# Dense networks: two pairs of steps by seven block products, with weight sums on GpSimd

## Chip, cores and metric

The kernel runs on 1 core of one Trainium2 chip. The metric is device microseconds (us) of one execution; lower is better.

## What is computed

Two transformer blocks over 256 tokens of width 1024, in float32. The first has a state space mixer, attention and a mixture of 32 experts; the second has two layers, each a dense network, a mixer, and a second dense network, so there are four dense networks in all. The change lies in those four:

```
def swiglu(x, w_gate, w_up, w_down):
    return (jax.nn.silu(x @ w_gate) * (x @ w_up)) @ w_down
...
    h = h + 0.5 * swiglu(rms_norm_2(h, ffn_norm[layer, 0]), ffn_w_gate[layer, 0], ffn_w_up[layer, 0], ffn_w_down[layer, 0])
```

`x` has 256 rows of 1024; the weights are 1024 x 2816, 1024 x 2816 and 2816 x 1024.

## The kernel before

**Steps.** A dense network q (0 to 3) is cut into 11 steps m (`FFN_STEPS`) of 256 hidden columns. Step m has one item of the ring: 128 partitions x 6144 columns, 3 MB, in three pieces of 2048 columns. Piece 0 and piece 1 hold the gate and up weights of the first and the second half of the 1024 inputs (each four blocks of 512 columns, 256 gate and 256 up), piece 2 holds the down weights.

**Split products.** Every factor is split into a high part and a low part (type fp32r), and `split_product` (line 2272) issues three matmuls of 512 columns: high x high, high x low, low x high (lines 2274, 2276 and 2275 in the profile). ScalarE makes the high part of a weight piece by a copy (`ffn_weights_high`, line 2896, profile line 2906), and DVE the low part by a subtraction with both operands in SBUF (`ffn_weights_low`, line 2833, by `low_part`, profile line 2280). High and low parts lie in the rooms of `ffn_hi` and `ffn_lo`, four rooms of 2048 columns each. In the text a form is the high and low part of one weight block.

**PE's order** (`ffn_tensor`, line 2735). `gate_up(m, 0)`, `gate_up(m, 1)`: 24 matmuls each, 8 blocks of 128 inputs x 2 token tiles x 3. `turn(m)`: four transposes of the gated rows (profile line 2785). `down(m)`: 24 matmuls that add to four banks held through the network. The loop is

```
        if m < FFN_LAST:
            gate_up(m + 1, 0)
            turn(m)
            gate_up(m + 1, 1)
        down(m)
```

**DVE and ScalarE** run hand-written orders of their own (`ffn_vector`, line 2841, and `ffn_scalar`, line 2909): per step three conversions, the silu on ScalarE (line 2920), the product with the up half on DVE (line 2854), and the split of the transposed rows (`turned_high`, line 2927, `turned_low`). Each engine runs its list in order and waits on semaphores, which count ends of instructions.

**Loads.** SyncE issues the items in the order of `plan_ring` (line 197) into three slots, item by item in turn. An item's load waits until the low part of the down weights of the item before it in that slot is made (`ffn_down_lo`). Loads and items keep that order into the next stage: after the first network come the entry weights `hy0`, `hy1`, after the second network the third one's items follow at once, and ScalarE and DVE make the third network's first form inside the second's last step.

**GpSimd** has little to do: it turns query and key rows (`mla_rows`, `nsa_query_rows`, `nsa_key_rows`; lines 724 to 730) in the mixers, and nothing in the dense networks.

**Last.** The gain of the last norm is loaded into `final_row`, 1024 columns of the tile `work`, after `out_ready` 12.

Of the kernel before, what the change touches and what calls it, by code (L numbers as in the profile page):

```python
# [56 lines left out]
FFN_STEPS = DFF2 // STEP_COLS  # L57
ALPHA = 1.702
# [42 lines left out]
def offsets(table):  # L101
# [80 lines left out]
def plan_ring(sig):  # L182
# [2537 lines left out]
def ffn_room(m, piece):  # L2720

    return 3 if piece == 2 and m == FFN_LAST else piece


def ffn_acts(k, part, m):

    return k[part if m < FFN_LAST else part.replace("act", "last")][:, :, :]


def down_free(q, m):  # L2730

    return downs_at(q, 0 if m == FFN_LAST else m)


def ffn_tensor(k, pe, q, nxt=None):
    s = k["sig"]
    base = FFN_STEPS * q
    half_kt = KT // 2

    def first_half():  # L2740
# [5 lines left out]
        def term(h, w):  # L2746
            for kt in range(half_kt):
                for t in range(TT):
                    mm = pe.matmul(k["ps"][2 * (base % 2) + t][:, :], k[h][:, kt, t * P:(t + 1) * P], k[w][:, 0, kt * 512:(kt + 1) * 512], start=h == "hT_hi" and w == "ffn_hi" and kt == 0, stop=False)  # L2749
            return mm  # L2750
# [3 lines left out]
        pe.wait_ge(s["ffn_w_lo"], 2 * base + 1)  # L2754
# [4 lines left out]
    def gate_up(m, piece):  # L2759
        n = base + m  # L2760
        pe.wait_ge(s["ffn_w_hi"], 2 * n + piece + 1)
# [3 lines left out]
        pe.wait_ge(s["ffn_w_lo"], 2 * n + piece + 1)  # L2765
# [4 lines left out]
        if piece == 0 and n >= 1:  # L2770
            pe.wait_ge(s["act_ready"], n)
        for kk in range(half_kt):
            kt = piece * half_kt + kk
            w = [k[part][:, piece, kk * 512:(kk + 1) * 512] for part in ("ffn_hi", "ffn_lo")]
            for t in range(TT):
                h = [k[part][:, kt, t * P:(t + 1) * P] for part in ("hT_hi", "hT_lo")]
                mm = split_product(pe, k["ps"][2 * (n % 2) + t][:, :], h, w, kt == 0, kt == KT - 1)
        mm.then_inc(s["gu_ready"], 1)

    def turn(m):  # L2780
        n = base + m
        pe.wait_ge(s["gu_drained"], n + 3)
        for ff in range(STEP_TILES):
            for t in range(TT):
                mm = pe.transpose(k["ps"][2 * (n % 2)][:, (ff * TT + t) * P:(ff * TT + t + 1) * P], k["sg"][:, t * STEP_COLS + ff * P:t * STEP_COLS + (ff + 1) * P], con(k, "ident"))  # L2785
        mm.then_inc(s["actT_ready"], 1)

    def down(m):
        n = base + m
# [27 lines left out]

    gate_up(0, 0)
    gate_up(0, 1)
    for m in range(FFN_STEPS):  # L2820
        if m < FFN_LAST:
            gate_up(m + 1, 0)
            turn(m)
            gate_up(m + 1, 1)
        down(m)


def downs_at(q, m):
# [12 lines left out]
def ffn_vector(k, dve, q, gain):
# [3 lines left out]
    def weights_low(m, piece):  # L2845
        ffn_weights_low(k, dve, q, m, piece)

    def swiglu(m):
        n = base + m
        banks = [k["ps"][2 * (n % 2) + t] for t in range(TT)]  # L2850
        dve.wait_ge(s["sig_ready"], n + 1)
        for t in range(TT):
            sg = k["sg"][:, t * STEP_COLS:(t + 1) * STEP_COLS]
            ins = dve.scalar_tensor_tensor(out=sg, in0=banks[t][:, STEP_COLS:2 * STEP_COLS], scalar=k["ss"][:, 4 + t:5 + t], in1=sg, op0=ALU.mult, op1=ALU.mult)
        ins.then_inc(s["gu_drained"], 1)

    def turned_low(m):
        n = base + m
        dve.wait_ge(s["actT_hi"], n + 1)
        low_part(dve, ffn_acts(k, "act_lo", m).rearrange("p a b -> p (a b)"), k["ps"][2 * (n % 2)][:, :], ffn_acts(k, "act_hi", m).rearrange("p a b -> p (a b)")).then_inc(s["act_ready"], 1)  # L2860

    i = FFN_NORM[q]
    if q == 0:
        ffn_norm_vector(k, dve, i, gain, 0)
        weights_low(0, 1)
    ffn_norm_vector(k, dve, i, gain, 1)
    weights_low(1, 0)
    token_scale_vector(k, dve, i)
    weights_low(1, 1)
    swiglu(0)  # L2870
    for m in range(FFN_STEPS):
        if m < FFN_LAST:
            weights_low(m, 2)
        turned_low(m)
        if m + 1 < FFN_LAST:
            weights_low(m + 2, 0)
            swiglu(m + 1)
            weights_low(m + 2, 1)
        elif m + 1 == FFN_LAST:
            weights_low(m + 1, 2)  # L2880
            if q == 1:
                ffn_weights_low(k, dve, 2, 0, 0)
            swiglu(m + 1)
            if q == 1:
                ffn_weights_low(k, dve, 2, 0, 1)
# [9 lines left out]

def ffn_weights_high(k, act, q, m, piece):
    s = k["sig"]
    n = FFN_STEPS * q + m
    it = k["plan"][f"ffn{q}_{m}"]
    act.wait_ge(k["landed"][it.slot], it.landed)  # L2900

    if piece == 2:
        act.wait_ge(s["down_done"], down_free(q, m))
    elif n >= 1:
        act.wait_ge(s["gu_ready"], 2 * (n - 1) + piece + 1)
    act.activation(k["ffn_hi"][:, ffn_room(m, piece), :], k["ring"][it.slot][:, piece * PIECE:(piece + 1) * PIECE], ACT.Copy).then_inc(s["ffn_down_hi"] if piece == 2 else s["ffn_w_hi"], 1)  # L2906


def ffn_scalar(k, act, q, gain, following=None):
# [3 lines left out]
    def weights_high(m, piece):  # L2913
        ffn_weights_high(k, act, q, m, piece)

    def sigmoid(m):
        n = base + m
        act.wait_ge(s["gu_ready"], 2 * n + 2)
        for t in range(TT):
            ins = act.activation(k["sg"][:, t * STEP_COLS:(t + 1) * STEP_COLS], k["ps"][2 * (n % 2) + t][:, 0:STEP_COLS], ACT.Silu, scale=k["ss"][:, 4 + t:5 + t])  # L2920
        ins.then_inc(s["sig_ready"], 1)

    def turned_high(m):
        n = base + m
        act.wait_ge(s["actT_ready"], n + 1)
# [1725 lines left out]
```

## Time and profile before

| | |
|---|---|
| median of 3 runs | 2247.02 us (2246.14 to 2247.46) |
| the profiled execution | 2244.58 us |
| its span, first to last instruction | 2242.8 us, 27250 instructions |
| PE busy | 2107.7 us, 94% |
| DVE busy | 1013.9 us, 45% |
| ScalarE (ACT) busy | 744.6 us, 33% |
| GpSimd (POOL) busy | 28.4 us, 1% |
| mean granted TensorE clock | 0.981 |

The profile is one execution, taken on the chip. Its own time stands 2.4 us below the median of the runs, and the sums below are made against it. A matmul is shown from its start to the end of its pipeline, so matmuls that follow each other overlap, and the work of PE is read from their starts. The granted clock is 1.00 at 2.4 GHz and 0.50 at 1.2 GHz. In a timeline "x4" means four instructions merged, and a bracket gives the idle time of the engine before an instruction and what released it.

### The profile page before, as it was taken

The numbers are of one execution on the slowest core, as the hardware profiler recorded it, in microseconds if no ns is written. First come the engines' busy times: TensorE is split into PE (matmuls) and PEld (weight loads), VectorE is DVE, ScalarE is ACT, GpSimd is POOL, SyncE is SP. The second block draws the span as 40 slices with busy tenths as digits, with TensorE's granted clock in tenths as the row PEclk, the third lists the DMA queues.
The fourth block names the chain that finished last, engine by engine and source line by source line (L and its number), as shares of the span: only waits on it lengthen the run. The fifth ranks groups of instructions, "written<-read, shape, count | busy, mean of one in ns | idle before, by whom it ended". The sixth has DMA issues, their size and how long they took to land.

```text
span 2242.8 us, 27250 instructions
## 1 busy us (share of the span) xinstructions
PE 2107.7 (94%) x11052; PEld 1296.3 (58%) x11052; DVE 1013.9 (45%) x1645; ACT 744.6 (33%) x1207; POOL 28.4 (1%) x38
## 2 busy tenths in 40 slices
PE   4989999998999999989877999999999999989998
PEld 3348743333333333333324888778888888867887
DVE  6975612222222212222215554775545545685545
ACT  6045321111111111111104444565445444375443
POOL 0000000000000000000000000100000000200000
PEclk9999889999999999999998999999999999999999
DMA  7773799999999999999997544435444543413441
GB/s 322 285 296 131 273 416 413 413 429 426 428 426 428 427 428 426 429 427 427 426 428 312 206 188 149 150 115 208 184 169 184 210 170 141 165 58 148 190 188 65
DMA packets 43506, 633.84 MB, mean 283 GB/s; under 512 B 5104, under 2 KB 5104, under 8 KB 6288
## 3 DMA queue, kind: packets, MB, share of 16 engines
q1 hardware_dynamic: 43376, 632.04, 68.6%
q8 instruction: 90, 1.47, 0.3%
q14 instruction: 40, 0.33, 0.0%
HBM read 630.97 MB, written 1.05 MB: 282 GB/s over the span
## 4 chain that ended last, share of the span: by engine, by line
PE 75%; DMA 16%; DVE 4%; ACT 4%; issue 1%; SPq 0%; DVEq 0%; ACTq 0%
DMA piece<-in_moe 15%; PE bank L2397 13%; PE bank L2274 13%; PE bank L2276 13%; PE bank L2275 13%; PE bank L2438 6%; PE bank L2372 3%; PE bank L2462 2%; PE bank L1027 2%; PE bank L2749 1%; PE bank L2785 1%; PE bank L340 1%; PE bank L714 1%; PE bank L2413 1%; DVE prob_n L1270 1%
## 5 line engine op out<-in xcount | busy, mean ns | idle before, releaser
L2397 PE MATMUL bank<-piece,xeT 128*64 128x512 f32 (+1 forms) x2304 | 449.3, 621 | 53.8 <-DMA piece<-in_moe 45.7
L2280 DVE TENSOR_TENSOR ffn_lo<-slot,ffn_hi 128x2048 fp32r<-128x2048 f32 x132 | 302.4, 2291 | 191.5 <-ACT ffn_hi L2906 191.5
L2397 PEld LDWEIGHTS bank<-piece,xeT 128*64 128x64 f32 (+1 forms) x2304 | 135.3, 131 | 334.0 <-issue 311.9
L2906 ACT ACTIVATE ffn_hi<-slot 128x2048 fp32r<-128x2048 f32 x132 | 252.2, 1913 | 125.9 <-PE bank L2276 114.7
L2274 PE MATMUL bank<-ffn_hi,hT_hi 128*128 128x512 f32 x672 | 265.6, 395 | 0.0
L2276 PE MATMUL bank<-ffn_hi,hT_lo 128*128 128x512 f32 x672 | 262.3, 390 | 0.0
L2275 PE MATMUL bank<-ffn_lo,hT_hi 128*128 128x512 f32 x672 | 261.6, 389 | 0.0
L2518 DVE TENSOR_TENSOR hT<-hT,bank 128x512 f32<-128x512 f32 x144 | 92.1, 681 | 254.2 <-PE bank L2462 254.0
L2567 DVE TENSOR_SCALAR work<-bank 128x256 f32<-128x256 f32 x60 | 25.5, 424 | 329.1 <-PE bank L2406 329.1
L2276 PEld LDWEIGHTS bank<-ffn_hi,hT_lo 128*128 128x128 f32 x672 | 126.1, 188 | 27.1
L2275 PEld LDWEIGHTS bank<-ffn_lo,hT_hi 128*128 128x128 f32 x672 | 126.3, 188 | 25.5
L2274 PEld LDWEIGHTS bank<-ffn_hi,hT_hi 128*128 128x128 f32 x672 | 126.4, 188 | 25.1
L2276 PE MATMUL bank<-ffn_hi,act_lo 128*128 128x512 f32 x320 | 127.0, 397 | 0.0
L2275 PE MATMUL bank<-ffn_lo,act_hi 128*128 128x512 f32 x320 | 126.7, 396 | 0.0
L2274 PE MATMUL bank<-ffn_hi,act_hi 128*128 128x512 f32 x320 | 124.9, 390 | 0.0
L2438 PE MATMUL bank<-piece,work 128*64 128x512 f32 (+1 forms) x528 | 108.7, 597 | 3.8 <-DMA piece<-in_moe 1.9
L2630 ACT ACTIVATE work<-bank 128x256 f32<-128x256 f32 x30 | 11.5, 384 | 288.5 <-PE bank L2413 288.5
L2462 PE MATMUL bank<-work 64*128 64x512 f32 x288 | 81.0, 640 | 1.2 <-ACT work L2651 1.2
L2372 PEld LDWEIGHTS bank<-ones,x 128*128 128x128 f32 x608 | 75.4, 206 | 9.8 <-issue 6.7
L2372 PE MATMUL bank<-ones,x 128*128 128x128 f32 (+1 forms) x608 | 78.1, 291 | 2.1 <-ACT hT L2256 1.2
L2920 ACT ACTIVATE work<-bank,ss 128x256 f32<-128x256 f32 x88 | 36.9, 472 | 121.8 <-PE bank L2276 121.8
L2622 ACT ACTIVATE xeT<-bank,fcol 128x128 f32<-128x128 f32 (+1 forms) x152 | 56.3, 450 | 47.2 <-PE bank L2372 47.2
(747 smaller groups left out, 2776.8 us busy)
## 6 DMA issues: line engine op xcount, KB each, us to landing
piece<-in_moe SPq DMA_DIRECT2D x190, 2048.0 KB, 26.5
slot<-in_ffn SPq DMA_DIRECT2D x44, 3072.0 KB, 10.3
slot<-in_ada SPq DMA_DIRECT2D x16, 1024.0 KB, 5.1
slot<-in_nsa_in SPq DMA_DIRECT2D x5, 2048.0 KB, 7.5
slot<-in_merge SPq DMA_DIRECT2D x3, 3072.0 KB, 13.3
slot<-in_ada SPq DMA_DIRECT2D x2, 3072.0 KB, 18.7
slot<-in_w_in SPq DMA_DIRECT2D x6, 1024.0 KB, 8.8
slot<-in_hy_in SPq DMA_DIRECT2D x3, 2048.0 KB, 7.7
```

What stands on the lines that cost most here:

```text
L1027: mm = pe.matmul(k["ps"][2 + u % 2][:, :], k["hT"][:, kt, t * P:(t + 1) * P], k["ring"][it.slot][:, lo:lo + 512], start=kt == 0, stop=kt = ...
L2274: pe.matmul(out, left[0], right[0], start=start, stop=False)
L2275: pe.matmul(out, left[0], right[1], start=False, stop=False)
L2276: return pe.matmul(out, left[1], right[0], start=False, stop=stop)
L2280: return dve.tensor_tensor(lo, x, hi.bitcast(F32), ALU.subtract)
L2372: mm = pe.matmul(k["ps"][4 + kt // 4][:, at + lo:at + hi], k["x"][:, t, kt * P:(kt + 1) * P], k["ones"][:, t, lo:hi], start=t == 0, stop=t ...
L2397: mm = pe.matmul(bank[n * c:n * (c + 1), :], x[:, kt, :], w[i][:, at:at + 512], start=kt == 0, stop=False)
L2438: mm = pe.matmul(bank[row:row + u.width, :], hid, piece[:, at:at + 512], start=e.begins and f == 0, stop=e.ends and f == 3)
L2462: mm = pe.matmul(k["ps"][base + half][:, :], k["shareT"][lo:lo + 64, t * P:(t + 1) * P], k["y_sb"][lo:lo + 64, :], start=True, stop=True)
L2518: ins = dve.tensor_tensor(total, total, k["ps"][base + half][:, :], ALU.add)
L2622: ins = act.activation(k["xeT"][:, q % 2, kt, lo:hi], k["ps"][4 + kt // 4][:, at + lo:at + hi], ACT.Identity, scale=router_gain(k, kt), bi ...
L2906: act.activation(k["ffn_hi"][:, ffn_room(m, piece), :], k["ring"][it.slot][:, piece * PIECE:(piece + 1) * PIECE], ACT.Copy).then_inc(s["ff ...
```

## The change

In each dense network steps 4 and 5 are taken together, and steps 8 and 9. The 256 x 1024 rows form a matrix A of 2 x 2 blocks (token tile x half of the inputs), the weights of the two steps a matrix B of 2 x 2 blocks (half of the inputs x step). The product of such matrices takes eight block products; here it is made by seven, with sums S1 to S4 of blocks of A and T1 to T4 of blocks of B, and the seven results are joined by additions:

```
+FFN_PAIRS = (4, 8)
+FFN_DOWNS = (0, 1, 2, 3, 5, 4, 6, 7, 9, 8, 10)
+FFN_BLOCKS = ("A11 B11", "S4 B22", "A12 B21", "S2 T2", "S1 T1", "S3 T3", "A22 T4")
+DOWN_ROOM = {0: 3, 1: 2, 2: 3, 3: 3, 5: 2, 4: 3, 6: 2, 7: 2, 9: 3, 8: 2, 10: 3}
```

A block product is four inputs blocks x three matmuls, 12 matmuls into one bank. PE's order around a pair (m, m + 1):

```
+    def pair(m):
+        a, b, c, d = pair_banks(k, q, m)
+        pe.wait_ge(s["act_ready"], base + m)
+        block(m, "A11 B11", a, True)
+        pe.wait_ge(s["ffn_joined"], 13 * q + 1)
+        block(m, "S4 B22", c, True)
+        turn(m - 1)
+        pe.wait_ge(s["ffn_kept"], kept_count(q, m, 1))
+        block(m, "A12 B21", a, False)
+        block(m, "S2 T2", b, True)
+        pe.wait_ge(s["ffn_kept"], kept_count(q, m, 2))
+        block(m, "S1 T1", c, True)
+        pe.wait_ge(s["ffn_joined"], joined_count(q, m, "U2"))
+        block(m, "S3 T3", b, False)
+        pe.wait_ge(s["act_ready"], base + m + 1)
+        block(m, "A22 T4", d, True)
...
+    for m in FFN_PAIRS:
+        pair(m)
+        down(m - 1)
+        turn(m + 1)
+        gate_up(m + 2, 0)
+        turn(m)
+        down(m + 1)
+        gate_up(m + 2, 1)
+        down(m)
+        if m + 3 < FFN_STEPS:
+            after_plain(m + 3)
+    down(FFN_LAST)
```

The forms of the seven blocks go through three rooms in turn (`spare`, 0, 1, `spare`, 0, 1, `spare`, where `spare` is the room of the down weights of m + 1), so a form may be written once the block three before it is done. DVE's order of a pair, and ScalarE's:

```
+    def pair(m):
+        low(m, "A11 B11")
+        turned_low(m - 2)
+        low(m, "S4 B22")
+        swiglu(m - 1)
+        low(m, "A12 B21")
+        low(m - 1)
+        low(m, "S2 T2")
+        turned_low(m - 1)
+        low(m, "S1 T1")
+        low(m, "S3 T3")
+        join(m, "U2")
+        low(m, "A22 T4")
+        for name in PAIR_JOINS[1:5]:
+            join(m, name)
+        low(m + 2, 0)
+        swiglu(m + 1)
+        join(m, "C21")
+        swiglu(m)
+        low(m + 1)
+        turned_low(m + 1)
+        low(m + 2, 1)
+        low(m)
+        turned_low(m)
...
+    def pair(m):
+        high(m, "A11 B11")
+        turned_high(m - 2)
+        high(m, "S4 B22")
+        silu(m - 1)
+        high(m, "A12 B21")
+        high(m - 1)
+        keep(m, 0)
+        high(m, "S2 T2")
+        keep(m, 1)
+        turned_high(m - 1)
+        high(m, "S1 T1")
+        high(m, "S3 T3")
+        high(m, "A22 T4")
+        high(m + 2, 0)
+        silu(m + 1)
+        silu(m)
+        high(m + 1)
+        turned_high(m + 1)
+        high(m + 2, 1)
+        high(m)
+        turned_high(m)
...
+    high(7, 0)
+    high(6)
+    silu(6)
+    high(7, 1)
+    pair(8)
+    high(FFN_LAST)
+    if q == 1:
+        ffn_weights_high(k, act, 2, 0, 0)
+    silu(FFN_LAST)
```

`high(m)` and `low(m)` with one argument are the down weights of step m; `keep` copies a bank to SBUF; `join` is one addition of 512 columns. The sums of A are made once per network on DVE while steps 1 to 3 run: the rows are put together from their parts (2048 columns), four sums of 512 columns are made, ScalarE copies their high parts (`sums_high`) and DVE makes their low parts (`sums_low`, just ahead of `pair(4)`). GpSimd makes the sums of B, T1 into the tile `behind`, the others over the weights in the slots:

```
+        for n in (m, m + 1):
+            it = k["plan"][f"ffn{q}_{n}"]
+            pool.wait_ge(k["landed"][it.slot], it.landed)
+        if m == FFN_PAIRS[0]:
+            pool.wait_ge(s["ffn_sum"], 4 * q + 4)
+        else:
+            pool.wait_ge(s["ffn_w_lo"], FFN_COUNT * q + FFN_FORMS[FFN_PAIRS[0], "S1 T1"])
+        pool.tensor_tensor(t1, b12, b11, ALU.subtract).then_inc(s["pair_sum"], 1)
+        pool.wait_ge(s["pair_sum"], sum_count(q, m, "T1"))
+        pool.tensor_tensor(b12, b22, b12, ALU.subtract).then_inc(s["pair_sum"], 1)
+        pool.wait_ge(s["ffn_w_lo"], FFN_COUNT * q + FFN_FORMS[m, "A11 B11"])
+        pool.tensor_tensor(t2, b22, t1, ALU.subtract).then_inc(s["pair_sum"], 1)
+        pool.wait_ge(s["pair_sum"], sum_count(q, m, "T2"))
+        pool.wait_ge(s["ffn_w_lo"], FFN_COUNT * q + FFN_FORMS[m, "A12 B21"])
+        pool.tensor_tensor(b21, t2, b21, ALU.subtract).then_inc(s["pair_sum"], 1)
```

In that order they are T1, T3, T2 and T4. The down product of step m + 1 goes ahead of that of step m (`FFN_DOWNS`), and a slot is given back after the low part of its down weights as before, in the new order. The load of the last gain waits for the down product of step 9 of the last network in place of `out_ready` 12, since the columns of `final_row` are in use until then. Five semaphores are merged into others (`gla_kdec` into `gla_pre`, `cmp_score` and `cmp_pT` into `cmp_kT`, `cmp_arg` into `cmp_p`), and four new ones are made.

## Rows read from the trace of the kernel before

**Rows 1.** The page, part 1: busy us (share of the span), instructions.
```profile
PE 2107.7 (94%) x11052; PEld 1296.3 (58%) x11052; DVE 1013.9 (45%) x1645; ACT 744.6 (33%) x1207; POOL 28.4 (1%) x38
```

**Rows 2.** Windows, one dense network; the columns are those of the header.
```profile
core 0: us, PE busy (x) PEld busy (x) DVE busy (x) ACT busy (x) POOL busy (x), PEclk, DMA share, GB/s
1512.00:1699.00 187.00, 186.88 (x848) 153.86 (x847) 96.68 (x76) 82.89 (x77) 0.00 (x0) 1.00 0.51 202
```

**Rows 3.** PE timeline: start, us, instruction; one step of the dense network.
```profile
1563.94 0.60 PE L2785 MATMUL bank<-consts,work 128*128 128x128 f32 x4
...
1569.87 0.39 PE L2274 MATMUL bank<-ffn_hi,act_hi 128*128 128x512 f32 x1
...
1575.42 0.39 PE L2274 MATMUL bank<-ffn_hi,hT_hi 128*128 128x512 f32 x1
...
1580.86 0.60 PE L2785 MATMUL bank<-consts,work 128*128 128x128 f32 x4
```

**Rows 4.** Groups by line, each shape apart: count, busy us, mean ns, idle before.
```profile
L2280 DVE TENSOR_TENSOR ffn_lo<-slot,ffn_hi 128x2048 fp32r<-128x2048 f32 x132 | 302.4, 2291 | 191.5 <-ACT ffn_hi L2906 191.5
...
L2906 ACT ACTIVATE ffn_hi<-slot 128x2048 fp32r<-128x2048 f32 x132 | 252.2, 1913 | 125.9 <-PE bank L2276 114.7 <-PE bank L2749 10.3 <-DVE ss L500 0.9
...
L2854 DVE SCALAR_TENSOR_TENSOR work<-bank,ss,work 128x256 f32<-128x256 f32 x88 | 38.5, 479 | 61.9 <-ACT work L2920 61.9
...
L2280 DVE TENSOR_TENSOR act_lo<-bank,act_hi 128x512 fp32r<-128x512 f32 x40 | 27.6, 690 | 79.6 <-ACT act_hi L2927 79.6
...
L2927 ACT ACTIVATE act_hi<-bank 128x512 fp32r<-128x512 f32 x40 | 24.0, 599 | 140.6 <-PE bank L2785 140.6
```

**Rows 5.** DMA issues by line: count, KB each, median us to landing.
```profile
slot<-in_ffn SPq DMA_DIRECT2D x44, 3072.0 KB, 10.3
...
work<-in_final_norm SPq DMA_DIRECT2D x1, 512.0 KB, 11.2
```

**Rows 6.** GpSimd (POOL) timeline in the third entry.
```profile
1924.50 1.27 POOL L725 TENSOR_TENSOR tmp_pool_n<-nq_n,sin 128x512 f32<-128x512 f32 x1
1925.73 3.31 POOL L726 TENSOR_TENSOR tmp_pool_n<-nq_n,cos 128x512 f32<-128x512 f32 x1
...
1930.35 1.29 POOL L729 TENSOR_TENSOR nq_n<-tmp_pool_n 128x512 f32<-128x512 f32 x1
```

**Rows 7.** DVE timeline of the same stretch.
```profile
1925.61 2.31 DVE L2280 TENSOR_TENSOR rest<-slot,end 128x2048 fp32r<-128x2048 f32 x1 [6.27 <-ACT end L656]
...
1930.19 0.33 DVE L3640 TENSOR_TENSOR hid_v_n<-hidT_n,bank 128x60 f32<-128x60 f32 x2
1930.45 3.34 DVE L2280 TENSOR_TENSOR rest<-slot,in_room_n 128x2048 fp32r<-128x2048 f32 x1
```

**Rows 8.** GpSimd timeline in the second entry.
```profile
1444.11 2.37 POOL L724 TENSOR_TENSOR tmp_pool_h<-mq_h,cos 128x128 f32<-128x128 f32 x1 [1443.66 <-DVE mkv_h L3136]
...
1449.32 0.46 POOL L727 TENSOR_TENSOR tmp_pool_h<-mq_h,sin 128x128 f32<-128x128 f32 x1
```

**Rows 9.** DVE timeline of the same stretch.
```profile
1443.88 2.28 DVE L2280 TENSOR_TENSOR rest<-slot,end 128x2048 fp32r<-128x2048 f32 x1
1446.08 2.55 DVE L2280 TENSOR_TENSOR rest<-slot,cat_hi_h 128x2048 fp32r<-128x2048 f32 x1
```

**Rows 10.** PE timeline before the first dense network; in brackets idle us before.
```profile
1170.61 4.84 PE L2397 MATMUL bank<-piece,xeT 128*32 128x512 f32 x28 [4.25 <-DMA piece<-in_moe]
```

**Rows 11.** Windows of 1 us after that idle time; columns as in group 2.
```profile
1170.00:1171.00 1.00, 0.39 (x4) 0.23 (x8) 0.00 (x0) 0.00 (x0) 0.00 (x0) 0.76 1.08 451
1171.00:1172.00 1.00, 1.00 (x8) 0.23 (x4) 0.00 (x0) 0.00 (x0) 0.00 (x0) 0.50 1.04 442
1172.00:1173.00 1.00, 1.00 (x8) 0.23 (x4) 0.00 (x0) 0.00 (x0) 0.00 (x0) 0.50 0.96 410
1173.00:1174.00 1.00, 1.00 (x12) 0.26 (x8) 0.00 (x0) 0.00 (x0) 0.00 (x0) 0.53 0.92 393
1174.00:1175.00 1.00, 1.00 (x16) 0.38 (x12) 0.00 (x0) 0.00 (x0) 0.00 (x0) 1.00 1.12 475
```

More of the change, by code:

```diff
@@ new lines, in ffn_acts, with acts_free, ffn_slot, ffn_plain @@
+def ffn_acts(k, part, m):
+    return k[part.replace("act", "last") if m in FFN_PAIRS else part][:, :, :]
+def acts_free(q, m):
+    same = [n for n in FFN_DOWNS if (n in FFN_PAIRS) == (m in FFN_PAIRS)]
+    at = same.index(m)
+    if at:
+        return down_ended(q, same[at - 1])
+    return down_ended(q - 1, same[-1]) if q else 0
+def ffn_slot(k, q, m):
+    return k["ring"][k["plan"][f"ffn{q}_{m}"].slot]
+def ffn_plain(k, q, what):
+    if isinstance(what, int):
+        return ffn_slot(k, q, what)[:, 2 * PIECE:3 * PIECE]
+    m, block = what
+    if isinstance(block, int):
+        return ffn_slot(k, q, m)[:, block * PIECE:(block + 1) * PIECE]
+    return {"B11": lambda: ffn_slot(k, q, m)[:, 0:PIECE], "B21": lambda: ffn_slot(k, q, m)[:, PIECE:2 * PIECE],
+            "B12": lambda: ffn_slot(k, q, m + 1)[:, 0:PIECE], "B22": lambda: ffn_slot(k, q, m + 1)[:, PIECE:2 * PIECE],
+            "T1": lambda: k["behind"][:, 0:PIECE], "T2": lambda: ffn_slot(k, q, m)[:, 0:PIECE],
+            "T3": lambda: ffn_slot(k, q, m + 1)[:, 0:PIECE], "T4": lambda: ffn_slot(k, q, m)[:, PIECE:2 * PIECE]}[block.split()[-1]]()
@@ new lines, in step_banks, with turn_back_bank, step_rows @@
+def step_banks(k, q, m):
+    lo = 2 * (FFN_PARITY[m] ^ q % 2)
+    return [k["ps"][lo + t] for t in range(TT)]
+def turn_back_bank(k, q, m):
+    if m in FFN_PAIRS:
+        return pair_banks(k, q, m)[0]
+    if m - 1 in FFN_PAIRS:
+        return pair_banks(k, q, m - 1)[2]
+    return step_banks(k, q, m)[0]
+def step_rows(k, q, m):
+    if m in FFN_PAIRS:
+        return [pair_banks(k, q, m)[0], k["behind"][:, 2560:3072]]
+    if m - 1 in FFN_PAIRS:
+        return [k["gate"], k["joined"][:, :]]
+    return step_banks(k, q, m)
@@ L2759, in gate_up @@
     def gate_up(m, piece):
[L2760 to L2761 removed]
+        form = first + FFN_FORMS[m, piece]
+        pe.wait_ge(s["ffn_w_hi"], form)
         if m == 0 and piece == 0:
@@ new lines, in block @@
+    def block(m, name, bank, fresh):
+        room, form = FORM_ROOM[m, name], first + FFN_FORMS[m, name]
+        pe.wait_ge(s["ffn_w_hi"], form)
+        pe.wait_ge(s["ffn_w_lo"], form)
+        for kk in range(half_kt):
+            w = [k[part][:, room, kk * 512:(kk + 1) * 512] for part in ("ffn_hi", "ffn_lo")]
+            mm = split_product(pe, bank[:, :], block_rows(name.split()[0], kk), w, fresh and kk == 0, kk == half_kt - 1, not fresh)
+        mm.then_inc(s["gu_ready"], 1)
+    def pair(m):
+        a, b, c, d = pair_banks(k, q, m)
+        pe.wait_ge(s["act_ready"], base + m)
+        block(m, "A11 B11", a, True)
[11 more added lines that the diff above has]
+        block(m, "A22 T4", d, True)
@@ L2864, in ffn_vector @@
         ffn_norm_vector(k, dve, i, gain, 0)
-        weights_low(0, 1)
+        low(0, 1)
     ffn_norm_vector(k, dve, i, gain, 1)
-    weights_low(1, 0)
+    low(1, 0)
     token_scale_vector(k, dve, i)
-    weights_low(1, 1)
+    low(1, 1)
     swiglu(0)
[L2871 to L2885, printed above, removed]
+    low(0)
@@ new lines, in keep, with pair @@
+    def keep(m, n):
+        form, bank = (("A11 B11", 0), ("S4 B22", 2))[n]
+        act.wait_ge(s["gu_ready"], FFN_COUNT * q + FFN_FORMS[m, form])
+        act.activation(k["behind"][:, 2048 + 512 * n:2560 + 512 * n], pair_banks(k, q, m)[bank], ACT.Copy).then_inc(s["ffn_kept"], 1)
+    def pair(m):
+        high(m, "A11 B11")
[19 more added lines that the diff above has]
+        turned_high(m)
```

371 lines of the change are left out of this document (273 added, 98 removed).

## Prediction

> **What bounds the kernel now.** I read the page's busy shares first: PE is busy 94% of the span [rows 1]. Then one dense network by itself: of 187 us PE is busy 186.88, at clock 1.00 [rows 2]. There is no wait to win in this stage, only PE work. The PE timeline of one step gives the price of that work. Busy times of matmuls overlap (each is shown as 0.39), so starts are what counts: 24 down products from 1569.87 to 1575.42 are 5.55, the next 24 gate/up products to 1580.86 are 5.44, so 0.2267 each; from one `turn` to the next is a step, 16.92 [rows 3]. The other engines have room: per step DVE runs three low parts (2.29), one small low part (0.69) and a swiglu pair (2 x 0.479), 8.5 us of 16.9; ScalarE three conversions (1.92), a copy (0.60) and the silu pair, about 7.3 [rows 4].
>
> **What is removed.** Per pair of steps 8 block products of 12 matmuls become 7; with 2 pairs in 4 networks that is 8 x 12 = 96 matmuls x 0.2267 = **-21.8 us**, or -5.44 per network, all on PE's path.
>
> **What is added, beside PE.** Per pair three more conversions on ScalarE (3 x 1.92) and two bank copies (2 x 0.60); on DVE three more low parts (3 x 2.29) and six joins (0.69 each, priced as the 512-column row); once per network one sum of 2048 columns (2.29) and eight of 512 (8 x 0.69). DVE gets about 30 us more in a network that leaves it 90 idle [rows 2]. I laid the new orders of PE, ScalarE, DVE, GpSimd and the loads out with these durations, hand-overs of 0.1 at most, and 10.3 from a load's issue to its landing [rows 5]; the same layout of the old order gives 16.93 per step. With GpSimd's sums at zero cost PE never waits in it: a room passes from block n to block n + 3, so a form (high and low part of one weight block) needs 1.92 + 2.29 = 4.2 and has the two blocks between, 2 x 12 x 0.2267 = 5.4. So those edits cost nothing, but what covers them is 1.2 us per form and no more.
>
> **GpSimd's sums.** Four subtractions of 128x2048 per pair: T1 and T3 when both steps' weights have landed, T2 after the low part of A11 B11, T4 after that of A12 B21. The trace has no such size. At 128x128 an undisturbed one takes 0.46, at 128x512 1.27 [rows 6, 8]: 0.81 for 384 columns, so 0.457 + 1920 x 0.00212 = **4.5 us** (an estimate). From below: DVE's 2.29 for the same shape [rows 4]; from above: four of 512, 5.1. I take 4.5, since both sizes lie on GpSimd itself. By the Trainium skill (GPSIMD Engine Reference, section 3.1) this operation takes 4.497, which no row here shows; the sum would be the same.
>
> They don't run beside DVE. A GpSimd sum that started at 1925.73, beside a DVE low part that ends at 1927.92, took 3.31 in place of 1.27 [rows 6, 7]. The other way round, GpSimd's of 1930.35 ended at 1931.64, and the low part recorded from 1930.45 took 3.34 in place of 2.29: it streamed from about 1931.50 (3.34 less 2.29 is 1.05 of waiting). Two short reads of a bank at 1930.19, beside the same GpSimd instruction, took 0.33 together. And at 1446.08 a low part queued right behind another let the waiting GpSimd instruction go first and took 2.55 [rows 8, 9]. So of two instructions that each read two SBUF operands one waits for the other, and they alternate. Every low part of weights is of that kind.
>
> By the Trainium skill (SBUF — State Buffer, "Who interferes with whom") the second fully blocks for the first's whole instruction. The rows let DVE go 0.15 before GpSimd's end; by the rule the sum below would be 5 us more.
>
> **First pair (steps 4, 5).** T1 and T3 come while DVE makes the low halves of the row sums (SBUF operands too): two of those wait 4.35 each, the low part of A11 B11 ends 8.5 late, and `turned_low(2)` behind it on DVE is late for down(2): PE waits 2.3. With t = 0 at the pair's first block: low part of A12 B21 until 3.5, low part of down(3) until 5.7, T4 (asked for at 3.6) 5.7 to 10.1, the low part of S2 T2 blocked until then, ending at 12.3. PE would start S2 T2 at 3 x 2.72 + 0.5 (the `turn`) = 8.7: it waits **3.6**.
>
> **Second pair (steps 8, 9).** Here the weights are late as well. Step 9's slot is step 6's, free after low(6), which ScalarE reaches behind high(7,0), which waits for step 7's load into step 4's slot. Counted from the end of pair (4, 5) on PE: down(3) frees step 4's room at 5.5, `turn(5)` follows; ScalarE's turned_high(5), high(6,1), high(4) end at 10.9 and DVE's low(6,1), low(4) at 13.2; load 7 lands at 23.5; high(7,0), high(6) end at 27.3, low(7,0), low(6) at 30.0; load 9 lands at 40.4. PE does four downs, four gate/up halves and three turns, 4 x 5.54 + 4 x 5.44 + 1.5 = 45.4. So T1 starts 5.0 before the pair: T1 -5.0 to -0.5; low part of S4 B22 to 1.7; T3 to 6.1; low part of A12 B21 to 8.3 (PE wanted it at 2 x 2.72 + 0.5 = 5.9: **2.4**); T2 to 12.7; low(7) to 14.8, while ScalarE, held in high(S2 T2) until T2 is there with the second bank copy and `turned_high(7)` queued behind it, converts it by 14.7; T4 to 19.3; low part of S2 T2 to 21.5, with `turned_low(7)` and the next two low parts queued behind it on DVE. PE was done with A12 B21 at 11.1: **10.4**. The rest of either pair runs at PE's pace (0.2 lost).
>
> Per network: -5.44 + 2.3 + 3.6 + 2.4 + 10.4 + 0.4 = **+13.7**.
>
> **The clock.** PE stood idle for 4.25 us before 1170.61 [rows 10]; the granted clock is then 0.76, 0.50, 0.50 and 0.53 in four slices of 1 us, and 1.00 again [rows 11]: 1.2 in place of 2.4 GHz for about 3.4 us, 1.7 us of work lost. Two of the four waits are of that size or longer: +3.4 per network (from below 0, if the clock holds).
>
> **Other moves.** Step 8's slot is now freed by low(8) behind low(9). At the end of the second network ScalarE and DVE issue the next network's first conversion ahead of silu(10) and swiglu(10); its load lands some 0.3 after silu(10) could run, and 1.92 + 2.29 stand ahead: the last `turn` is 2.8 late, once. In the first and third network that conversion stands behind silu(10), and its load (from 21 us before the end) is hidden. The final gain's load waits for down(9) of the last network: downs 8 and 10, half a gate/up and a `turn`, some 17 us of PE, remain, and it landed in 11.2 [rows 5]. The merged semaphores keep their order: 0.
>
> **Sum.** 4 x (13.7 + 3.4) + 2.8 = +71.2. The profiled execution took 2244.58 (span 2242.8), 2.4 below the median of 2247.02: 2315.8 there, **2318** against the median, 3% slower.
>
> **Rivals.**
> *No exclusion* (no change): GpSimd streams beside DVE. Then only the second pair waits: T1 to T2 are 3 x 4.5 from -5.0, so T2 is there at 8.8, S2 T2 at 13.2 instead of 8.7: 4.6. Per network -0.7, in all about 2247. Against it: the stretched instructions [rows 6 to 9]. Chance 0.08.
> *GpSimd is quick enough* (faster): no exclusion at this size, and a sum of 2048 columns at 3.0 or less, so that T2 beats its need at 8.7 less 4.2. Then nothing waits: -21.8 + 2.8 = -19, 2228. It decides at T2's end against 4.5 us into the pair. For it: GpSimd's instructions in the trace have 512 columns at most and cannot show a long one's pace. Against it: two sizes give 0.0021 per column, nearly twice the 0.0011 that 3.0 asks for beyond 512, and the exclusion. Chance 0.12.
> *The exclusion holds, but milder* (slower, less): at 3.5 a sum and no clock loss the same layout gives +5.7 per network, 2273; at 4.0, +9.7, 2289. At DVE's own 2.29 it gives -1.2, 2245, and counts as no change. Where T1 and T3 met nothing and T2 and T4 alone cost, the first pair's 3.6 twice gives +1.8 per network, 2257. All but the one at 2.29 lie inside the forecast's case.
>
> **Chances and range.** Slower 0.80, same 0.08, faster 0.12; I call 0.2%, 4.5 us, what a measurement of this kernel can tell from nothing. The forecast's own bounds: 2273 as above to 2341 (5.1 a sum, DVE held to GpSimd's end, clock lost: +22.7 per network, + 2.8). To hold 8 in 10 the range goes a little past both: 2262 to 2345.
>
> **What would show it.** In the changed profile: 24 more low parts of 2048 columns on DVE, some of 6.6 us instead of 2.29, GpSimd's subtractions at 4.5 and many at 6.5; PE idle before S2 T2 in every second pair by some 10 us with DVE's low part as releaser, by 3 to 4 in every first; no PE idle elsewhere in the networks; 96 matmuls fewer. Wrong if DVE's low parts stay at 2.29 while GpSimd runs, if a sum takes under 3.5, or if the weights of step 9 land more than 10 us before the pair.

## The result and the profile after

The changed kernel took **2320.39 us** (median of 4 runs, 2319.74 to 2321.46) against 2246.71 (2246.14 to 2247.46) for the kernel before on the same chip: ratio **1.0328, 95% interval 1.0313 to 1.0344**. It is 3.3% slower; the forecast was 2318. The profiled execution took 2321.46, its span is 2319.7 us. One execution is left out of all figures below: of the kernel with the sums on DVE, one took 5348 us where the other three took 2259 to 2266.

The page of the changed kernel, part 1 (to be read against [rows 1]):

```profile
PE 2113.0 (91%) x10956; PEld 1293.2 (56%) x10956; DVE 1243.4 (54%) x1753; ACT 806.4 (35%) x1263; POOL 205.2 (9%) x70
```

PE has 96 matmuls fewer, as the change says, and is busy for longer. DVE has 108 instructions more and 229.5 us more of busy time. The groups by line tell where that is (count, busy us, mean ns, idle before):

```profile
L2287 DVE TENSOR_TENSOR ffn_lo<-slot,ffn_hi 128x2048 fp32r<-128x2048 f32 x148 | 429.0, 2916 | 148.8 <-ACT ffn_hi L3236 148.3
...
L3211 POOL TENSOR_TENSOR slot<-slot 128x2048 f32<-128x2048 f32 x8 | 48.1, 6011 | 21.4 <-DVE ffn_lo L2287 21.1
L3206 POOL TENSOR_TENSOR slot<-slot 128x2048 f32<-128x2048 f32 x8 | 46.0, 5752 | 0.6
L3208 POOL TENSOR_TENSOR slot<-slot,behind_ring 128x2048 f32<-128x2048 f32 x8 | 44.8, 5601 | 11.3 <-DVE ffn_lo L2287 11.3
L3204 POOL TENSOR_TENSOR behind_ring<-slot 128x2048 f32<-128x2048 f32 x8 | 38.4, 4794 | 1825.1 <-DMA slot<-in_ffn 1825.1
```

The mean low part rose from 2.29 [rows 4] to 2.92 us; GpSimd's four sums (L3204 T1, L3206 T3, L3208 T2, L3211 T4) have means of 4.8 to 6.0. A mean hides what happens, so here is one second pair (steps 8 and 9) by time, first GpSimd, then DVE (start, us, instruction, idle before):

```profile
1346.95 4.64 POOL L3204 TENSOR_TENSOR behind_ring<-slot 128x2048 f32<-128x2048 f32 x1 [55.38 <-DMA slot<-in_ffn]
1351.66 6.55 POOL L3206 TENSOR_TENSOR slot<-slot 128x2048 f32<-128x2048 f32 x1
1358.18 6.61 POOL L3208 TENSOR_TENSOR slot<-slot,behind_ring 128x2048 f32<-128x2048 f32 x1
1364.87 6.45 POOL L3211 TENSOR_TENSOR slot<-slot 128x2048 f32<-128x2048 f32 x1
```

```profile
1348.80 4.94 DVE L2287 TENSOR_TENSOR ffn_lo<-slot,ffn_hi 128x2048 fp32r<-128x2048 f32 x1 [5.87 <-ACT ffn_hi L3236]
1353.66 0.86 DVE L3072 SCALAR_TENSOR_TENSOR work<-bank,ss,work 128x256 f32<-128x256 f32 x2
1354.45 19.03 DVE L2287 TENSOR_TENSOR ffn_lo<-slot,ffn_hi 128x2048 fp32r<-128x2048 f32 x3
```

The first sum, which has nothing ahead of it, takes 4.64; with a low part in between the sums follow each other every 6.5 to 6.7 us, and three low parts take 19.03 in place of 6.9 (3 x 2.29). `swiglu` (L3072), which reads a bank, goes through at its usual pace beside a sum. PE's waits (us in total, times, the longest), then GpSimd's T1 in the second pair of the second network, and PE's timeline at the four waits of that network and at its last `turn`:

```profile
PE bank L2281 <- DVE ffn_lo L2287: 58.9, 12, 10.1
PE bank L2281 <- DVE act_lo L2287: 9.2, 4, 2.3
...
PE bank L2986 <- DVE work L3072: 4.0, 1, 4.0
```

```profile
1661.02 4.64 POOL L3204 TENSOR_TENSOR behind_ring<-slot 128x2048 f32<-128x2048 f32 x1 [55.10 <-DMA slot<-in_ffn]
```

```profile
1590.17 0.47 PE L2281 MATMUL bank<-ffn_hi,act_hi 128*128 128x512 f32 x1 [2.29 <-DVE act_lo L2287]
...
1608.21 0.47 PE L2281 MATMUL bank<-ffn_hi,xn_lo 128*128 128x512 f32 x1 [3.57 <-DVE ffn_lo L2287]
...
1674.58 0.77 PE L2281 MATMUL bank<-ffn_hi,hT_hi 128*128 128x512 f32 x1 [2.36 <-DVE ffn_lo L2287]
...
1687.67 0.77 PE L2281 MATMUL bank<-ffn_hi,xn_lo 128*128 128x512 f32 x1 [8.59 <-DVE ffn_lo L2287]
...
1730.26 1.12 PE L2986 MATMUL bank<-consts,work 128*128 128x128 f32 x4 [3.98 <-DVE work L3072]
```

These are 72.1 us of waits that the kernel before doesn't have, each with a late DVE as releaser. In every network they stand before down(2), before S2 T2 of the first pair, and before A12 B21 and S2 T2 of the second; the fifth, before a `turn`, comes once. From the start of T1 to the first product of S2 T2 a second pair takes 26.7 us in all four networks (here 1661.02 to 1687.67). The mean granted clock fell from 0.98 to 0.965.

The stages, each from the first product of a dense network to that of the next (or to the end of the span), in us, for four kernels. Of these e7_fill is the experiment "What the clock costs" and e6_dve_order "The sums on DVE, in an order that fits":

```
network (and what follows it)   before   changed   e7_fill   e6_dve_order
first                           298.53    314.10    313.84         293.82
second                          188.15    212.15    207.12         185.64
third                           347.15    365.36    361.64         343.53
fourth                          194.92    211.76    208.97         190.79
sum                            1028.75   1103.37   1091.57        1013.78
```

From the first network on the loss is 74.6 us. Counted from a network's first product to its last, 73.0 of it lie inside the networks: 15.6, 24.0, 16.6 and 16.8. The other 1.6 come in what follows the third. The waits less the 21.8 us of products saved leave 50.3. Most of what is missing to 73.0 is the clock: behind these waits PE worked some 40 us at 0.50, by the clock records of this trace, which is about 20 us of work lost.

### The profile page after: what moved, and what is told of

It is laid out like the page before. It is cut to its first block, busy times and chain, and to the rows that moved or that the text cites. A ratio compares the mean times of both kernels' runs of the same rounds, so it can differ in the third digit from the quotient of the medians.

```text
span 2319.7 us, 27338 instructions
## 1 busy us (share of the span) xinstructions
PE 2113.0 (91%) x10956; PEld 1293.2 (56%) x10956; DVE 1243.4 (54%) x1753; ACT 806.4 (35%) x1263; POOL 205.2 (9%) x70
## 4 chain that ended last, share of the span: by engine, by line
PE 60%; DMA 19%; DVE 15%; ACT 5%; issue 1%; SPq 0%; ACTq 0%; DVEq 0%
DMA piece<-in_moe 15%; PE bank L2404 13%; DVE ffn_lo L2287 9%; PE bank L2281 9%; PE bank L2282 8%; PE bank L2283 8%; PE bank L2445 6%; DMA slot<-in_ffn 3%; PE bank L2379 2%; ACT ffn_hi L3236 2%; PE bank L2469 2%; PE bank L1034 2%; DVE work_r L2287 1%; DVE hT_first L2287 1%; PE bank L2916 1%
## 5 line engine op out<-in xcount | busy, mean ns | idle before, releaser
L2287 DVE TENSOR_TENSOR ffn_lo<-slot,ffn_hi 128x2048 fp32r<-128x2048 f32 x148 | 429.0, 2916 | 148.8 <-ACT ffn_hi L3236 148.3
L3236 ACT ACTIVATE ffn_hi<-slot 128x2048 fp32r<-128x2048 f32 x148 | 281.3, 1913 | 251.2 <-PE bank L2283 133.8
L2281 PE MATMUL bank<-ffn_hi,hT_hi 128*128 128x512 f32 x512 | 203.1, 397 | 8.4 <-DVE ffn_lo L2287 8.4
L2283 PE MATMUL bank<-ffn_hi,hT_lo 128*128 128x512 f32 x512 | 200.2, 391 | 0.0
L2282 PE MATMUL bank<-ffn_lo,hT_hi 128*128 128x512 f32 x512 | 200.0, 391 | 0.0
L3204 POOL TENSOR_TENSOR behind_ring<-slot 128x2048 f32<-128x2048 f32 x8 | 38.4, 4794 | 1825.1 <-DMA slot<-in_ffn 1825.1
L2281 PEld LDWEIGHTS bank<-ffn_hi,hT_hi 128*128 128x128 f32 x512 | 96.7, 189 | 28.4 <-issue 9.2
L2283 PEld LDWEIGHTS bank<-ffn_hi,hT_lo 128*128 128x128 f32 x512 | 96.5, 188 | 20.6
L2282 PEld LDWEIGHTS bank<-ffn_lo,hT_hi 128*128 128x128 f32 x512 | 96.7, 189 | 19.4
L2281 PE MATMUL bank<-ffn_hi,xn_lo 128*128 128x512 f32 x128 | 55.7, 435 | 50.6 <-DVE ffn_lo L2287 50.6
```

The lines of the kernel that those rows point to most:

```text
L2281: pe.matmul(out, left[0], right[0], start=start, stop=False, skip_group_check=again)
L2282: pe.matmul(out, left[0], right[1], start=False, stop=False, skip_group_check=again)
L2287: return dve.tensor_tensor(lo, x, hi.bitcast(F32), ALU.subtract)
L3204: pool.tensor_tensor(t1, b12, b11, ALU.subtract).then_inc(s["pair_sum"], 1)
L3236: act.activation(k["ffn_hi"][:, room, :], ffn_plain(k, q, what), ACT.Copy).then_inc(s["ffn_down_hi"] if isinstance(what, int) else s["ffn_ ...
```

## The experiments

Each was run beside the kernel before on the same chip, whose medians there were 2247 to 2248 us.

### No long sums

```diff
-        pool.tensor_tensor(t1, b12, b11, ALU.subtract)
+        pool.tensor_tensor(k['behind'][:, 0:64], b12[:, 0:64], b11[:, 0:64], ALU.subtract)
...
```

> GpSimd's sums are cut to 64 columns and written aside; the forms T1 to T4 are made from plain weight blocks instead, so the sums themselves are left out. Theory (the sums of 2048 columns hold up DVE's low parts): every PE wait in the pairs goes, about 66 us of waits and the clock loss behind them; what is left against the kernel before is 96 matmuls less (-21.8) and the late last turn of the second network (4 of wait and about 3 of clock): 2228 to 2240 us. Rival (the seven-block order with its three rooms and joins is too much for DVE even without the sums): more than 5 us of PE waits per network stay in front of blocks of the pairs, 2260 us or more.

Measured: 2230.68 us, one run. No wait before a product of the pairs is left, and no low part is stretched (group mean 2289 ns). So the joins, the additional forms and the new order of the queues cost PE nothing in the pairs, and the loss there hangs on the sums. From the first network on the kernel is 14.9 us under the kernel before, not 21.8: the late `turn` at the end of the second network is still there (4.4 us and a fall of the clock behind it).

### GpSimd busy, without reading

```diff
-        pool.tensor_tensor(t1, b12, b11, ALU.subtract)
+        k['pos'].mark(pool.memset(t1, 0.0))
+        k['pos'].wait()
+        pool.memset(t1, 0.0)
...
```

> Each of GpSimd's sums becomes two fills of the same 2048 columns, one after the other, which read nothing from SBUF; the sums are left out (the T blocks are zero). Theory (the exclusion is between instructions that read two SBUF operands): DVE's low parts stay at 2.29 while GpSimd runs, no low part of 4 us or more; with fills of together 4.0 to 4.8 us only the second pair's S2 T2 waits, 3 to 5.5 us, 2242 to 2265 us. Rival A (late weights and the length of the chain T1 to T2 make the time, no exclusion needed): about 2310 to 2320 if the fills are as long as the sums. Rival B (GpSimd excludes DVE whatever it does): low parts of 4 to 6.6 us again, about 2305 to 2320.

Measured: 2242.86 us, one run. Timelines of a second pair, GpSimd (first two of eight fills) and DVE:

```profile
1340.54 1.81 POOL L3204 MEMSET behind_ring<- 128x2048 f32 x1 [56.31 <-DMA slot<-in_ffn]
1342.41 1.81 POOL L3206 MEMSET behind_ring<- 128x2048 f32 x1
```

```profile
1342.41 2.29 DVE L2287 TENSOR_TENSOR ffn_lo<-slot,ffn_hi 128x2048 fp32r<-128x2048 f32 x1 [6.25 <-ACT ffn_hi L3244]
1344.62 0.87 DVE L3072 SCALAR_TENSOR_TENSOR work<-bank,ss,work 128x256 f32<-128x256 f32 x2
1345.41 2.28 DVE L2287 TENSOR_TENSOR ffn_lo<-slot,ffn_hi 128x2048 fp32r<-128x2048 f32 x1
1347.90 2.29 DVE L2287 TENSOR_TENSOR ffn_lo<-slot,ffn_hi 128x2048 fp32r<-128x2048 f32 x1 [0.22 <-ACT ffn_hi L3244]
```

GpSimd is at work without a gap from 1340.54 to 1355.3, with its output in the same places, and the low parts beside it keep 2.29. So it is not that GpSimd is busy, nor that it writes, that holds DVE up. In each network one wait of 1.2 to 2.5 us is left, before S2 T2 of the second pair, where the weights land as late as before (T1 starts 4.1 to 5.5 us ahead of the pair).

One reservation: two fills are 3.7 us, a sum 4.6, so a part of the gain is that GpSimd is done sooner. An estimate of that part: from T1's start to S2 T2's first product are 15.5 us here and 26.7 with the sums. A sum is 0.95 longer than two fills, from start to start, and T1, T3 and T2 stand in this chain: 15.5 would become some 18.4. So about 8 of the 11 us between the two are the exclusion. No run has GpSimd at work for 4.6 us at a time without reading.

### A copy in place of the sum

This run was made to test the words "two instructions that each read two SBUF operands" of the forecast.

```diff
-        pool.tensor_tensor(t1, b12, b11, ALU.subtract)
+        pool.tensor_copy(t1, b12)
...
```

> The changed kernel with each of GpSimd's sums replaced by a copy of its first operand into the same place (128x2048, one operand read from SBUF in place of two); the differences are left out, so T1 to T4 hold plain blocks. All waits and the order stay. Theory (two instructions exclude each other only where each reads two operands from SBUF): low parts beside the copies keep 2.29 us, and what is left is GpSimd's own length, of which the trace shows no copy of this size: by layout 2231 us at 3.5 us a copy, 2244 at 4.5, 2256 at 5.5. Rival (any read of SBUF by GpSimd shuts VectorE's two-operand reads out): low parts of 5 to 7 us beside the copies as in the change, and 2285 us or more at 4.5 us a copy. What counts is the longest low part (2.4 against over 4 us) rather than the time.

Measured: 2239.94 us, one run. The same timelines, GpSimd and DVE:

```profile
1337.63 1.90 POOL L3204 COPY behind_ring<-slot 128x2048 f32<-128x2048 f32 x1 [57.53 <-DMA slot<-in_ffn]
1339.59 3.96 POOL L3206 COPY slot<-slot 128x2048 f32<-128x2048 f32 x1
1343.50 3.95 POOL L3208 COPY slot<-behind_ring 128x2048 f32<-128x2048 f32 x1
1347.51 3.84 POOL L3211 COPY slot<-slot 128x2048 f32<-128x2048 f32 x1
```

```profile
1339.50 2.29 DVE L2287 TENSOR_TENSOR ffn_lo<-slot,ffn_hi 128x2048 fp32r<-128x2048 f32 x1 [5.70 <-ACT ffn_hi L3236]
1341.71 0.87 DVE L3072 SCALAR_TENSOR_TENSOR work<-bank,ss,work 128x256 f32<-128x256 f32 x2
1342.49 11.00 DVE L2287 TENSOR_TENSOR ffn_lo<-slot,ffn_hi 128x2048 fp32r<-128x2048 f32 x3
```

The theory as I had put it falls. A copy reads one operand, takes 1.90 by itself and 3.9 beside low parts; three low parts take 11.0, the longest 3.98, which is 2.29 and a copy less 0.2. They alternate just as the sums did, and from T1's start to S2 T2's first product are 16.0 us in all four networks. The time, 2239.94, lies where the theory put it, but only because a copy is so short. So it is enough that GpSimd **reads** SBUF at all while DVE reads two operands there; the fills show that writing does no harm.

The Trainium skill has it so (SBUF — State Buffer, "Who interferes with whom"): a DVE instruction with two SBUF inputs contends with a GpSimd instruction that reads SBUF, not with one that only writes it. Both halves agree with these two runs.

### The weights of step 6 earlier

```diff
-    high(7, 0)
     high(6)
+    high(7, 0)
     silu(6)
...
```

and the same on DVE.

> The down weights of step 6 are converted ahead of the first half of step 7, so that the slot of step 9 is free and its weights land earlier (by 2 to 10 us, as the loads before it allow). Theory (exclusion): T1 and T3 start earlier, the wait before A12 B21 (2.2) shrinks or goes, but T2 and T4 still alternate with low(7) and the low part of S2 T2, whose wait stays at 9 us or more: 2 to 3 us per network, 2308 to 2313 us. Rival (late weights): the wait before S2 T2 shrinks by as much as the landing moves, 2 to 10 us per network beside the 2.2: 2270 to 2305 us.

Measured: ratio 1.0304 (1.0287 to 1.0321), 2312.5 to 2316.7 us. Two waits of one second pair (PE timeline):

```profile
1355.84 0.47 PE L2281 MATMUL bank<-ffn_hi,hT_hi 128*128 128x512 f32 x1 [0.42 <-DVE ffn_lo L2287]
...
1368.95 0.77 PE L2281 MATMUL bank<-ffn_hi,xn_lo 128*128 128x512 f32 x1 [10.11 <-DVE ffn_lo L2287]
```

The wait before A12 B21 shrank from 2.0 to 0.4, the long one stayed at 10.1. The median, 2315.34, is above the 2308 to 2313 of the theory. The weights came only a little earlier, not 2 to 10 us: T1 starts 1.0 to 1.7 us earlier against the pair's first product. S2 T2 starts earlier by the same amount, and the way from one to the other is again 26.7 us:

```profile
1342.28 4.63 POOL L3204 TENSOR_TENSOR behind_ring<-slot 128x2048 f32<-128x2048 f32 x1 [53.82 <-DMA slot<-in_ffn]
```

So late weights do count: they set when T1 starts, and the wait before A12 B21 took up all of the small shift. How far the wait before S2 T2 would shrink under a larger one, this run does not show. That late weights alone make the loss is ruled out by the fills and the copies: there T1 starts as late, 4.1 to 5.7 us ahead of the pair, and the pairs' waits are 2.5 us at most.

### The end of the second network

```diff
     high(FFN_LAST)
-    if q == 1:
-        ffn_weights_high(k, act, 2, 0, 0)
     silu(FFN_LAST)
...
```

The forms of the next network come behind this one's own work, on ScalarE and on DVE.

> At the end of the second network the third network's first two forms are moved behind silu(10), swiglu(10) and the split of the last transposed rows; all else as changed. Theory: the wait of 4.0 us before the last turn goes, and with it the stretch of low clock behind it (about 3 us): about 2313 us, 7 less than the changed kernel. Rival (the forms are then late at the start of the third network, which gives the time back there): 2317 to 2321.

Measured: ratio 1.0309 (1.0292 to 1.0327), median 2315.96, so 4.4 us less than the changed kernel and between the two theories. In the trace the wait of 3.98 before that `turn` is gone; one of 1.3 (`PE bank L587 <- DVE x`) came at the start of what follows. Taken from the start of the second network to that of the fourth the gain is 6.4 us, close to the 7 expected; the fourth network then took 1.7 us more than in the changed kernel, though nothing in this edit touches it. So 1 or 2 us of a stage are not told apart by one profile of each.

### What the clock costs

Products whose results are overwritten, in place of idling: 9 before down(2), 15, 9 and 43 before the three blocks of the pairs that wait.

```diff
+    def fill(bank, n):
+        rows = k["hT_hi"][:, 0:2, :].rearrange("p a b -> p (a b)")
+        for _ in range(n):
+            pe.matmul(bank[:, :], k["hT_hi"][:, 0, 0:P], rows, start=True, stop=True)
...
         block(m, "A12 B21", a, False)
+        fill(b, 15 if m == FFN_PAIRS[0] else 43)
         block(m, "S2 T2", b, True)
```

> The changed kernel, with products added whose results are overwritten: 9 ahead of down(2), 15 ahead of S2 T2 of the first pair, 9 ahead of A12 B21 and 43 ahead of S2 T2 of the second, each 128x128 by 512 columns (0.227 us) from parts already there, so that TensorE works through nearly all of each wait (2.0, 3.4, 2.0 and 9.8 us) instead of idling. Theory (behind the waits the granted clock falls and costs some 25 us over the four networks, beside the waits themselves): the 0.50 stretches behind these waits go, TensorE's busy time rises by 69 us less what the low clock cost, and the time falls by 15 to 25 us, to 2295 to 2306. Rival (the low clock costs nothing, since the next form is late anyway and sets the pace): 2316 to 2324. If the added products themselves are on the path: over 2325.

Measured: 2308.94 us, one run, between the two theories' ranges. The first of the changed kernel's waits and the windows of 1 us around its end show what there was to win (columns as in [rows 2]; the clock is the third number from the end):

```profile
1277.78 0.47 PE L2281 MATMUL bank<-ffn_hi,act_hi 128*128 128x512 f32 x1 [2.33 <-DVE act_lo L2287]
```

```profile
1277.00:1278.00 1.00, 0.22 (x1) 0.25 (x2) 1.00 (x3) 1.00 (x1) 0.89 (x1) 1.00 0.00 0
1278.00:1279.00 1.00, 1.00 (x4) 0.75 (x4) 1.00 (x1) 0.12 (x1) 1.00 (x1) 0.73 0.00 0
1279.00:1280.00 1.00, 1.00 (x4) 0.77 (x3) 1.00 (x1) 0.00 (x0) 1.00 (x1) 0.50 0.00 0
1280.00:1281.00 1.00, 1.00 (x4) 0.80 (x3) 1.00 (x1) 0.00 (x0) 1.00 (x1) 0.50 0.00 0
1281.00:1282.00 1.00, 1.00 (x4) 0.77 (x4) 1.00 (x1) 0.00 (x0) 0.67 (x1) 0.56 0.00 0
```

After a wait of only 2.33 us PE ran at 0.50, the level of 1.2 GHz, for some 3.5 us. With the products added, no slice under 0.98 is left in the first network behind these waits, nor in the second's pairs, and the clock of the whole span rises from 0.965 to 0.979. From the first network on that gave 1103.4 - 1091.6 = **11.8 us**: 0.3, 5.0, 3.7 and 2.8 by stage, from one profile of each kernel. It is less than the 20 us that the slow stretches hold because a wait follows: PE that comes late to S2 T2 waits less there. After the fall shown the wait before S2 T2 was 2.21, without one 3.57 (second network). Of the 5.0 in the second stage a part is at the late `turn`, whose wait is 2.4 in place of 4.0.

### The sums on DVE

```diff
+        sum_of(m, "T1")
         low(m, "A11 B11")
         turned_low(m - 2)
         low(m, "S4 B22")
+        sum_of(m, "T2")
+        sum_of(m, "T3")
         swiglu(m - 1)
         low(m, "A12 B21")
+        sum_of(m, "T4")
```

> All four sums of both pairs are made by VectorE at 2.29 us each (the price of a low part), T1 ahead of the low part of A11 B11, T2 and T3 behind the one of S4 B22, T4 behind the one of A12 B21; GpSimd makes none. Nothing else is changed, 48 products of each pair still fall away. Theory (GpSimd's sums and the low parts exclude each other, and a sum on GpSimd costs 4.5 us of a time in which VectorE does nothing): the waits before down(2), S2 T2 of the first pair and S2 T2 of the second go, but VectorE now has 18.3 us more to do in each network and is late elsewhere: laid out by hand, 5.8 us before down(6) and 2.1 us before S2 T2 of the second pair, with 1.7 us of low clock behind each. 4 x (5.8 + 2.1 + 3.4 - 5.44) = +23 us on before, about 2270 us, 50 us under the change; no low part over 2.4 us. Rival (VectorE has no room for the sums; it sets the pace through the whole pair): over 2300 us. Rival (the sums cost nothing wherever they are, and the loss comes from the joins and the order): within 10 us of the change.

Measured: ratio 1.0055 (1.0037 to 1.0073), 2259.4 to 2265.6 us: some 60 us under the changed kernel (1.0055 x 2247.8 is 2260, against 2320.4), with the same four sums per pair, and 10 under the 2270 expected. In the profile the groups of these sums (L3150) have means of 2284 to 2287 ns, and the low parts are at 2287 again. Of the two waits that the layout gave, one came:

```profile
PE bank L2281 <- DVE act_lo L2287: 21.2, 4, 5.5
```

That is 5.3 us before down(6) in each network, since T1 of the second pair stands ahead of `turned_low(6)` on DVE and waits for step 9's weights. The 2.1 expected before S2 T2 did not come.

### The sums on DVE, in an order that fits

```diff
+        if m == FFN_PAIRS[0]:
+            sum_of(m, "T1")
+            low(m, "A11 B11")
+        else:
+            low(m, "A11 B11")
+            sum_of(m, "T1")
...
         low(m + 1)
+        if m == FFN_PAIRS[0]:
+            low(m)
+            turned_low(m + 1)
+            low(m + 2, 1)
+            low(m + 2)
+            turned_low(m)
...
```

The parts of down(4) and down(6) are moved alike on ScalarE, and the end of the second network is that of the experiment "The end of the second network".

> The sums on VectorE as in the run before, and the order mended where that layout leaves waits: of the first pair the parts of down(4) are formed right behind those of down(5), the parts of (6) ahead of those of (7,0), the low part of A11 B11 of the second pair ahead of its T1, and the forms of the third network made in the last step of the second come behind that step's own work. Theory: no wait over 0.5 us is left before a product of the pairs in any network, the 96 products (21.8 us) are all gain but for some waits of under half a microsecond (about 0.7 us per network): 2228 us, range 2224 to 2240, under both kernels. Rival (the joins and the seven-block order cost by themselves, some 5 us per network): 2245 or more. Rival (VectorE has no room): over 2260.

Measured: **2232.81 us** (2229.64 to 2235.1, 5 runs), ratio **0.9934 (0.9921 to 0.9948)**: faster than both kernels and within the expected range. The profile is of its fastest execution, 2229.64. DVE's timeline of a second pair:

```profile
1336.06 2.28 DVE L2287 TENSOR_TENSOR ffn_lo<-slot,ffn_hi 128x2048 fp32r<-128x2048 f32 x1
1338.26 2.28 DVE L3150 TENSOR_TENSOR slot<-slot,behind_ring 128x2048 f32<-128x2048 f32 x1
1340.46 2.28 DVE L3150 TENSOR_TENSOR slot<-slot 128x2048 f32<-128x2048 f32 x1
1342.66 0.87 DVE L3072 SCALAR_TENSOR_TENSOR work<-bank,ss,work 128x256 f32<-128x256 f32 x2
1343.45 2.28 DVE L2287 TENSOR_TENSOR ffn_lo<-slot,ffn_hi 128x2048 fp32r<-128x2048 f32 x1
```

and PE's waits for low parts:

```profile
PE bank L2281 <- DVE ffn_lo L2287: 3.7, 4, 1.1
```

A sum takes 2.28 and is followed at once by the next instruction. One wait of 0.8 to 1.1 us is left per network (I expected none over 0.5), before S2 T2 of the second pair, and the clock doesn't fall behind it.

## Why the forecast was right

- **-21.8 for the products.** 96 matmuls fewer, as said. Where nothing waits, in the kernel without long sums, the first, third and fourth networks are each 5.3 to 5.5 us shorter, against 5.44.
- **The price of a sum, 4.5 us.** Undisturbed ones take 4.6. The Trainium skill gives 4.497 for an addition of this size (GPSIMD Engine Reference, section 3.1); the trace's subtractions, 4.56 to 4.64, are 1 to 3% above.
- **The exclusion.** Right in what it does here, too narrow in its reason: GpSimd's reading is enough, it need not read two operands. The rows of before had GpSimd instructions with two operands only and could not tell. For a sum the two wordings give the same. Whoever would have put a GpSimd copy into this stage by the forecast's rule would have been wrong.
- **How long it locks.** A low part and a sum follow each other every 6.5 to 6.7 us, 0.2 to 0.4 less than 4.6 + 2.29. The forecast's value, which lets DVE go a little before GpSimd's end, was nearer than the whole instruction. The Trainium skill (SBUF — State Buffer, "SBUF: two separate sides") has the second blocked for the whole of the first; these rows show it blocked for all but the last 0.2 to 0.4 us, of which 0.08 is the overlap that DVE's instructions have in the records anyway (2.28 each, 2.20 apart).
- **The four waits.** 2.3, 3.6, 2.4 and 10.4 were laid out; the changed kernel has 2.3, 2.2 to 3.6, 1.8 to 2.4, and 8.6 to 10.1. In the second pair of the first network A12 B21 went on 8.1 us and S2 T2 21.2 us after the pair's first product (1352.45); the layout had 8.3 and 21.5. T1 started 5.1 to 5.7 ahead of the pair, where the layout had 5.0, and the chain from there to S2 T2 took 26.7 against 26.5. This is the mechanism of the forecast, step by step, and not luck. Over four networks the waits are 68.1 us (58.9 + 9.2) against 74.8 laid out. Most of the difference belongs to the clock: PE at 1.2 GHz came late to the next wait. The forecast's list of signs names only the waits before S2 T2 and no others; its own layout has the other two.
- **The clock, 13.6.** Its net price is 11.8, part of it at the late `turn`. That the two come so close is partly luck. I had one row, a fall behind 4.25 us of idling, and counted two falls per network although only one of the four waits is that long. The clock fell behind waits of 2.3 too, and in other places did not; it cost some 20 us of work, of which shorter waits behind it gave a part back; and by stage the net is 0.3 to 5.0, not 3.4 in each.
- **The late `turn`, 2.8.** It was 4.0, and the clock then stayed at 0.50 for some 6 us: 6.4 us by the run that takes it away. This term was less than half of what it measured, and makes the second network the one that loses 24. In the sum it errs the other way from the waits and the clock, so that the total came nearer than its parts.
- **The rivals.** *No exclusion* and *quick enough* fall with the changed trace; the run without long sums is what the second would have looked like (2228 was said, 2231 measured). *Milder* falls with the undisturbed 4.6.

## What to carry to other kernels

Work moved from a half idle VectorE to an idle GpSimd is not free when it reads SBUF and VectorE's own instructions read two operands there: while a GpSimd sum of 4.6 us runs, such an instruction of VectorE waits, and VectorE would have made the sum itself in 2.3. Compare that lost time with the price on the busy engine before asking which one has room. And when an engine gets more work, its order has to be laid out again: the same sums on VectorE lost 0.5% in the order at hand and won 0.7% in one where no late load stands ahead of what is wanted next (the mended end of the second network included).

## What the chip showed that I had not expected

A GpSimd copy of 128x2048 takes 1.90 us and a fill 1.81, against 4.6 for the subtraction; the copy and the subtraction hold up VectorE's two-operand reads, the fill does not.

The granted clock fell to 0.50 behind one wait of 2.29 us and stayed at 1.00 behind another of 2.29, both before down(2): the one that ends at 1590.17 in the second network (above), and this one in the third. First the product behind it, then a slice of 1 us behind each, second network and third:

```profile
1802.84 0.47 PE L2281 MATMUL bank<-ffn_hi,act_hi 128*128 128x512 f32 x1 [2.29 <-DVE act_lo L2287]
```

```profile
1591.00:1592.00 1.00, 1.00 (x6) 0.83 (x5) 1.00 (x1) 0.00 (x0) 1.00 (x1) 1.00 0.00 0
1805.00:1806.00 1.00, 1.00 (x4) 0.80 (x3) 1.00 (x1) 0.00 (x0) 1.00 (x1) 0.50 0.00 0
```

What tells them apart was not tried.
